# State-space head loop: the backward diagonal's bias moved from ScalarE's exponentials to an add on GpSimd

## What is computed

```python
dt = softplus(dt + dt_bias); log_a = dt * (-exp(a_log))
# per head, chunk by chunk, scalar decay
g_cum = cumsum(log_a)
rel = exp(where(causal, g_cum[i] - g_cum[j], -inf))
scores = einsum('bhik,bhjk->bhij', c, b * dt) * rel
o = scores @ v + (c * exp(g_cum)) @ state
```

## Time and profile before

| | us |
|---|---|
| median of three runs | 2350.61 (2348.07 to 2355.66) |
| the profiled execution | 2356.56 |
| its span in the trace | 2354.8 |

### The profile page before, as it was taken

One profiled execution on the slowest core, in us unless ns is written; L12 is line 12 of the kernel. 1 busy time (PEld: TensorE's weight loads), 2 busy tenths in 40 slices (PEclk: granted clock), 3 DMA queues, 4 the chain that ended last, 5 costly groups with the idle time before them and its releaser, 6 DMA issues.

```text
span 2354.8 us, 32702 instructions
## 1 busy us (share of the span) xinstructions
PE 2277.3 (97%) x11907; PEld 1964.0 (83%) x11907; DVE 1374.7 (58%) x1750; ACT 905.9 (38%) x1979; POOL 1056.1 (45%) x815
## 2 busy tenths in 40 slices
PE   7999999999889999999999999999999999999998
PEld 6999999998438999999999998976455568888887
DVE  5985878853765457857857466664568654111113
ACT  5215434443892356756746252232321213101002
POOL 3353334324542345544535433455133135766664
PEclk9999999999889999999999999999999999999999
DMA  8953334254631134434534423354132213333332
GB/s 278 314 160 115 106 119 140 79 177 142 201 103 36 55 114 128 144 108 125 151 100 129 76 79 125 113 185 139 59 108 93 68 47 92 95 97 98 98 96 83
DMA packets 392724, 281.07 MB, mean 119 GB/s; under 512 B 33442, under 2 KB 357820, under 8 KB 392604
## 3 DMA queue, kind: packets, MB, share of 16 engines
q1 hardware_dynamic: 333420, 200.46, 28.7%
q10 hardware_dynamic: 59184, 78.99, 9.9%
HBM read 237.34 MB, written 42.07 MB: 119 GB/s over the span
## 4 chain that ended last, share of the span: by engine, by line
PE 81%; DVE 9%; ACT 5%; DMA 2%; issue 1%; POOL 0%; SPq 0%; ACTq 0%; DVEq 0%; POOLq 0%
PE PS L962 54%; PE PS L1045 4%; PE PS L1654 4%; PE PS L1483 3%; PE PS L1495 3%; PE PS L1606 2%; PE PS L1140 1%; PE PS L1305 1%; DVE Gn L2560 1%; PE PS L1106 1%; DVE stage L2516 1%; PE PS L1124 1%; ACT Dm L2056 1%; DVE xcr L2516 1%; PE PS L1555 1%
## 5 line engine op out<-in xcount | busy, mean ns | idle before, releaser
L962 PE MATMUL PS<-act_hi,w_hi 128*128 128x384 f32 (+1 forms) x1824 | 638.5, 350 | 6.3 <-ACT act_hi L2117 2.8
L962 PE MATMUL PS<-act_hi,w_lo 128*128 128x384 f32 (+1 forms) x1824 | 630.7, 346 | 0.0
L962 PE MATMUL PS<-act_lo,w_hi 128*128 128x384 f32 (+1 forms) x1824 | 627.3, 346 | 0.0
L744 POOL TENSOR_TENSOR w_hi<-w_raw,ones 128x128 fp32r<-128x128 f32 x232 | 128.3, 553 | 1064.5 <-DMA w_raw<-in_ffn_w 404.5
L747 POOL TENSOR_TENSOR w_lo<-w_raw,w_hi 128x1024 fp32r<-128x1024 f32 (+1 forms) x232 | 559.8, 2413 | 19.4
L962 PEld LDWEIGHTS PS<-act_hi,w_hi 128*128 128x128 f32 x1824 | 343.6, 188 | 28.6 <-issue 11.6
L962 PEld LDWEIGHTS PS<-act_lo,w_hi 128*128 128x128 f32 x1824 | 343.9, 189 | 15.3 <-issue 1.2
L962 PEld LDWEIGHTS PS<-act_hi,w_lo 128*128 128x128 f32 x1824 | 343.6, 188 | 13.7
L2132 ACT ACTIVATE fprod<-mf_ring,cs 128x128 f32<-128x128 f32 x896 | 267.9, 388 | 26.5 <-DVE mf_acc L2431 26.5
L2431 DVE TENSOR_REDUCE mf_acc<-fprod 128x128 f32<-128x1024 f32 x112 | 225.0, 2021 | 85.9 <-ACT fprod L2132 85.9
L745 POOL TENSOR_SCALAR w_hi<-w_raw 128x896 fp32r<-128x896 f32 (+1 forms) x232 | 234.2, 1010 | 0.0
(11 more groups left out here) (376 smaller groups left out, 3695.1 us busy)
## 6 DMA issues: line engine op xcount, KB each, us to landing
w_raw<-in_ffn_w SPq DMA_DIRECT2D x120, 512.0 KB, 3.9
mf_ring<-in_w_mod SPq DMA_DIRECT2D x56, 512.0 KB, 3.7
w_raw<-in_a_w_in SPq DMA_DIRECT2D x44, 512.0 KB, 4.2
proj<-stage ACTq DMA_DIRECT2D x44, 384.0 KB, 4.2
w_raw<-in_b_w_up SPq DMA_DIRECT2D x32, 512.0 KB, 4.6
m_ring<-in_w_mod SPq DMA_DIRECT2D x12, 1024.0 KB, 9.0
rows<-g_d SPq DMA_DIRECT2D x16, 768.0 KB
m_raw<-in_w_mod SPq DMA_DIRECT2D x4, 2048.0 KB, 11.8
```

The costliest lines, as they stand in the source:

```text
L744: pool.tensor_tensor(w_hi[:, s, 0], w_raw[:, s, 0], ones[:], ALU.mult)
L962: last = pe.matmul(to[:, c0:c1], w[:, s, k, :], x[:, k, c0:c1], start=k == 0 and w is w_hi and x is hi, stop=k == kt - 1 and w is w_lo)
```

## The change

GpSimd first adds the column terms of the backward direction to the row terms, over all 768 columns, into `Db`. Each column term is read as one number repeated 128 times. A wait on GpSimd's own semaphore (`chain`) stands between this add and the select, which now works in place on `Db`. At head 0 GpSimd also waits until `nb` is written. ScalarE then takes one exponential over the 768 columns of `Db`, without a bias. The forward direction is left as it was.

```diff
                         if h >= 2:
                             pool.wait_ge(fb_done, h - 1)
-                        pool.affine_select(out=diagonals(Db[:, h % 2], 0, 6, P), in_=row[:, 1].rearrange("p (c t) -> p c t", t=P),
+                        if h == 0:
+                            pool.wait_ge(ct_put, 1)
+                        b = Db[:, h % 2].rearrange("p (c t) -> p c t", t=P)
+                        chain(pool.tensor_tensor(b, row[:, 1].rearrange("p (c t) -> p c t", t=P),
+                                                 nb[:, 1, :, 16 + h:17 + h].broadcast_to([P, 6, P]), ALU.add))
+                        pool.affine_select(out=b, in_=b,
                                            compare_op=ALU.is_ge, fill=-1e30, base=0, pattern=[[0, 6], [-1, P]],
                                            channel_multiplier=1).then_inc(back_mask, 1)
...
             def backward_decays(h):
                 b = Db[:, h % 2]
                 act.wait_ge(back_mask, h + 1)
-                for c in range(6):
-                    act.activation(b[:, c * P:c * P + P], b[:, c * P:c * P + P], ACT.Exp, bias=nb[:, 1, c, 16 + h:17 + h])
+                act.activation(b, b, ACT.Exp)
```

## The result

The changed kernel takes 2357.43 us (median of 19 runs) against 2352.54 for the kernel before, timed alongside. The ratio is 1.0028 with a 95% interval of 1.0016 to 1.0041, that is +6.6 us with +3.8 to +9.6. The forecast was +12. The sign held, the size was 1.8 times too large. The profiled execution took 2360.43 us (span 2358.7).

A forecast was written before the change was run, and what follows sets the result against it. ScalarE bounds the head loop now; with the add, GpSimd and VectorE together would. Terms +6.3, +2.1 to +4.8, +3.6, -1.0 and 0 gave +11.0 to +13.7, taken as +12: 2362.6 us, range 2343 to 2371.

The forecast's parts named there:

- ScalarE's gain: Six backward exponentials a head become one on ScalarE: 0.98 us a head, beyond head 0 lost waiting for GpSimd.
- Head 0's -1.0: Head 0's exponentials lie on the chain and get 0.98 us shorter, so what follows comes earlier: -1.0 us.
- The shared resource: GpSimd's operations and VectorE's with two SBUF inputs run one after the other: 5.59 us a head, 7.42 with the add.
- the queue: The add lengthens GpSimd's own queue and delays ScalarE; priced in the first rival at 1.83 us, for head 3 alone.
- the beginning: Around head 2, new adds, split and head 3's select delay head 2's multiply from 609.27 to 612.9: +3.6 us.
- The size of the add: GpSimd's new add over 768 columns was taken as 1.83 us, like a plain add, plus some 0.05 of wait.
- The sum from head 2 to head 15: Between these multiplies, 13 heads x 7.42 plus split and adds of squares give 105.7 us against 99.42: +6.3.
- Idle time: At the change of group neither engine can work for 4.8 us; head 10's add and select may fit: +2.1 to +4.8.
- The tail: Behind head 15's multiply everything stays as before: 0 us.
- The first: Rival: the add doesn't hold VectorE up or fits into its waits: -7 us, 2343.6; chance 0.20 including what lies between.
- The pace of 7.06 as the point of decision: Second rival, 2340 us, chance 0.10: decides once shared work per head falls under 7.06, with under 1.47 us of add.

The follow-up runs named there:

- e1: Kernel before with one ScalarE exponential over 768 columns, no add on GpSimd, backward column terms left out: -8.2 us against before.
- e2: Changed kernel with ScalarE back at six exponentials a head, GpSimd's add kept: +6.1 us against the kernel before.
- e3: Kernel of e1 with two GpSimd constant fills (768 and 576 columns) ahead of the select: -1.4 us against the kernel before.
- e7: Kernel before with add and single exponential only for heads 0, 1, 4, 7, 9, 13 and 15: -6.1 us against before.
- e11: The same kernel as e7, timed again: -7.5 us against the kernel before.
- e5: Changed kernel with the weight splits behind heads 2 and 5 moved behind heads 9 and 15: +1.9 us against the kernel before.
- e6: Kernel before with the weight splits behind heads 2 and 5 moved behind heads 9 and 15: +0.5 us against before.
- e9: Kernel of e7 with the weight splits behind heads 2 and 5 moved behind heads 9 and 15: -1.2 us against the kernel before.
- e8: Kernel before with add and single exponential for even heads alone, two weight splits moved behind heads 9 and 15: -2.6 us against before.
- e12: Kernel of e7 with head 10 in place of head 15 for add and single exponential: -2.8 us against the kernel before.
- e4: Changed kernel with forward row terms, a plain operand, in place of the add's repeated column: +8.2 us against the kernel before.

## Why the prediction was right in sign and too large

- *ScalarE's gain.* Forecast 0.98 us a head; the exponential over 768 columns is recorded at 0.84 and its successor starts 0.75 behind it. Right. That it would be lost behind GpSimd: right, shown by e1 and e2. Head 0's -1.0: from VectorE's first residual sum of this region to its first multiply it was 15.9 us and is 14.9 (568.58 to 583.47), right.
- *The shared resource.* Right as a mechanism: e3 shows it with the read taken away. Its share was overstated, since the prediction gave the queue nothing beyond the beginning. The fills, which only lengthen the queue, cost 4.4 us of loop and 6.8 of total (e3).
- *The size of the add failed.* The step "nothing in the trace lets such an operand cost less than a plain one" took 1.83 us and bounded it from below there. It is 1.48, with 0.15 instead of 0.05 for the wait. In the sum 7.42 us a head should have been 7.22: 13 x 0.20 = 2.6 us too much. A bound was set on one side alone, where the trace showed nothing of such an operand at all.
- *The sum from head 2 to head 15* was the second term mis-sized: one head is counted twice. With 7.22 it would give 13 x 7.22 + 3.75 + 5.5 = 103.1 us, +3.7; measured are 104.4 (611.32 to 715.71), +5.0. That looks close, but the 13 turns take in GpSimd's add and select for head 3, which the term for the beginning already has. In the trace head 3's select is under way at 611.15 when the stretch begins, and up to 715.71 there are 12 adds and 12 selects, for heads 4 to 15, beside 13 pairs of masks. Counted so it is 13 x 3.81 + 12 x (1.63 + 0.82) + 13 x 0.96 + 3.75 + 5.5 = 100.7 us. In the forecast's prices the double count is 1.83 + 0.82 = 2.65 us.
- *Idle time.* 104.4 - 100.7 leaves 3.7 us, within the forecast's +2.1 to +4.8. It is a balance of two things. From head 7 to head 10, around the change of group, 28.6 us pass (649.36 to 677.97) and the operations that stand there add up to 22.6, so 6.0 are idle. From head 2 to head 7 the sum gives too much, 5 x 7.22 + 3.75 = 39.9 against 38.04 (611.32 to 649.36), and from head 10 to head 15 38.2 against 37.7. A reading of the latter that no run tests: at each hand-over a little of an operation's recorded time lies outside the exclusive part.
- *The beginning.* Forecast +3.6, with the order of operations around 609 us exactly as it came. Head 2's multiply starts 2.05 us later, of which 0.4 is the shift of head 1's, and is recorded 0.46 longer since the select holds it: about +2.1. The shorter add accounts for 0.4 of the difference, as two of them stand there.
- *The tail.* Forecast 0. The last pair's output product comes 11.0 us behind head 15's multiply in before (719.68) and 11.5 in the changed kernel (727.25), where VectorE's next operation with two SBUF inputs meets an addition of squares on GpSimd and is recorded at 2.42 us instead of 0.96: +0.5.
- Together: the forecast's 12 were 6.3 and some 3.1 for the stretch from head 2 to head 15, 3.6 for the beginning and -1.0 for head 0. The trace shows 5.0, 1.7 (start to start), -1.0 and 0.5 for the tail, 6.2 in all, against 6.6 in the timed runs. Of the 4.4 us between 9.4 and 5.0, 2.4 are the shorter add in 12 turns, 2.65 the head counted twice, and -0.6 the idle time. So the mechanism held, and the price of the add, the double count and the beginning were off, all to the same side.
- *The rivals.* The first, that the add finds its place, fell for all heads at once; for seven chosen ones the kernel is faster by as much as this rival had (e7, e11), though the loop shows only a part of it. The pace of 7.06 as the point of decision was too simple: e2, with a shared work of 7.2 and ScalarE at 7.06, is 6 us slower than before. My reading, not tested by itself, is that two resources that are each nearly full don't mesh.

## What to carry to other kernels

Before work goes from a bound engine to one with a low share, add up what that engine and whoever shares a port with it do within one turn of the loop, and look at what already stands in its queue ahead of the moved step: here a resource of 5.6 us in a pace of 7.06 had room for a new 1.6 in some turns and not in all. An idle stretch of GpSimd is a free slot only if VectorE doesn't have work on two SBUF operands there: the moved splits met such work in e5, e6 and e9. And when a sum by turns is put together with a term for the beginning, check that no turn's work stands in both. Where a move doesn't pay for every turn, try it for some: seven heads of 16 was the only complete version whose gain is clear of zero. That slack is the right way to choose them is plausible but not shown (e8, e9, e12).

## What the runs showed of the hardware

- GpSimd's add over 768 columns takes 1.48 us with a second operand that repeats one number 128 times, and 1.80 to 1.84 us with a plain one (e4); the forecast had taken them to be alike.
- GpSimd's fills, which read nothing, ran under VectorE's multiply of two SBUF operands at their usual length (0.73 and 0.58 us, the multiply at 2.91 against 2.83, e3), while the select behind them, which reads SBUF, took 1.94 us instead of 0.86. The Trainium skill, SBUF — State Buffer, section Who interferes with whom, says so: a VectorE instruction with two SBUF inputs contends with a GpSimd instruction that reads SBUF, not with one that only writes. The trace agrees.
- An ACTIVATE without a given bias over 768 columns is recorded at 0.84 us, as long as the squares of that width (0.83).
